# Last attention in blocks of 32 columns by four rows with 176 keys, its bias tables on GpSimd's queue, and a new order at the two ends of the state-space pipeline

## What is computed

```python
rows = S // GRID_W                    # 256 // 64 = 4
kh = min(NA_KH, rows)                 # 4: every query sees all four rows
col_start = np.clip(col - kw // 2, 0, GRID_W - kw)        # kw = 16 columns of each
col_mask = (col[None, :] >= col_start[:, None]) & (col[None, :] < col_start[:, None] + kw)
s = jnp.einsum("bqhd,bjkhd->bhqjk", q_row, k_rows) * scale + bias
s = jnp.where(col_mask[None, None, :, None, :], s, -jnp.inf)
p = jax.nn.softmax(jnp.concatenate([s, s_m], axis=-1), axis=-1)   # s_m: the 16 meta keys
```

## Time and profile before

| | us |
|---|---|
| median of 3 runs (lowest, highest) | 2495.55 (2494.72, 2496.42) |
| the profiled execution | 2496.76 |
| its span, first to last instruction | 2494.7 |
| mean granted clock | 0.994 |

### The profile page before, as it was taken

The page is one execution under the profiler, slowest core; times in us unless marked ns, Lnnn a source line. Parts: engine busy times, 40 slices in busy tenths (PEclk is TensorE's granted clock), DMA queues, the critical chain, the costliest instruction groups (busy, mean ns, idle before and its releaser), DMA issues.

```text
span 2494.7 us, 53545 instructions
## 1 busy us (share of the span) xinstructions
PE 2451.5 (98%) x18774; PEld 2342.1 (94%) x18774; DVE 1808.0 (72%) x3175; ACT 1173.0 (47%) x1663; POOL 580.5 (23%) x366
## 2 busy tenths in 40 slices
PE   8999999999999999989999999999999999999997
PEld 8999899999999888889999999999999999999986
DVE  6877877777777655578888878888862676666765
ACT  5444444444444444455666633333544444444443
POOL 0400000000000000033324257777777110001100
PEclk9999999999999999999999999999999999999999
DMA  8544655555555666665545545555455645545544
GB/s 275 189 165 136 209 170 186 184 186 184 186 184 194 195 186 186 199 207 160 181 161 166 173 138 175 174 171 193 170 169 176 187 158 168 169 158 164 166 138 140
DMA packets 159417, 441.32 MB, mean 177 GB/s; under 512 B 39475, under 2 KB 54236, under 8 KB 159212
## 3 DMA queue, kind: packets, MB, share of 16 engines
q1 hardware_dynamic: 156156, 428.15, 52.2%
q0 software_dynamic: 3184, 12.14, 1.6%
HBM read 438.05 MB, written 11.09 MB: 180 GB/s over the span
## 4 chain that ended last, share of the span: by engine, by line
PE 79%; DVE 9%; issue 5%; ACT 4%; DMA 1%; DVEq 1%; POOL 1%; ACTq 0%; SPq 0%; POOLq 0%
PE bank L1069 19%; PE bank L1070 19%; PE bank L1071 19%; PE bank L1064 10%; PE bank L1065 5%; DVE wlo L1495 3%; ACT whi L608 2%; PE bank L1302 1%; PE bank L1413 1%; ACT cv L781 1%; ACT cg L781 1%; PE bank L1394 1%; DVE cg L1802 1%; DVE cg L1805 1%; DVE cv L1802 1%
## 5 line engine op out<-in xcount | busy, mean ns | idle before, releaser
L1069 PE MATMUL bank<-xhl,whi 128*128 128x256 f32 (+1 forms) x4492 | 1294.3, 288 | 7.0 <-POOL wlo L563 3.3
L1070 PE MATMUL bank<-xhl,whi 128*128 128x256 f32 (+1 forms) x4492 | 1282.4, 285 | 0.0
L1071 PE MATMUL bank<-xhl,wlo 128*128 128x256 f32 (+1 forms) x4492 | 1281.5, 285 | 0.0
L608 ACT CAST whi<-raw 128x1024 fp32r<-128x1024 f32 x784 | 810.6, 1044 | 649.9 <-PE bank L1071 527.8
L1495 DVE TENSOR_TENSOR wlo<-raw,whi 128x1024 fp32r<-128x1024 f32 x624 | 766.6, 1239 | 239.1 <-ACT whi L608 235.2
L1069 PEld LDWEIGHTS bank<-xhl,whi 128*128 128x128 f32 x4492 | 851.0, 189 | 17.6 <-issue 9.5
L1071 PEld LDWEIGHTS bank<-xhl,wlo 128*128 128x128 f32 x4492 | 851.0, 189 | 0.0
L1070 PEld LDWEIGHTS bank<-xhl,whi 128*128 128x128 f32 x4492 | 848.5, 189 | 0.8 <-issue 0.2
L563 POOL TENSOR_TENSOR wlo<-raw,whi 128x1024 fp32r<-128x1024 f32 x160 | 383.5, 2405 | 141.5 <-ACT whi L608 141.4
L1064 PE MATMUL bank<-fhl,whi 128*128 128x512 f32 x928 | 329.5, 399 | 0.3 <-DVE wlo L1495 0.3
L1065 PE MATMUL bank<-fhl,wlo 128*128 128x256 f32 x960 | 264.4, 281 | 0.0
(11 more groups left out here) (278 smaller groups left out, 2530.4 us busy)
## 6 DMA issues: line engine op xcount, KB each, us to landing
raw<-w_up SPq DMA_DIRECT2D x176, 512.0 KB, 4.1
raw<-w_na SPq DMA_DIRECT2D x128, 512.0 KB, 3.5
raw<-w_ssm SPq DMA_DIRECT2D x96, 512.0 KB, 3.5
raw<-w_glu SPq DMA_DIRECT2D x96, 512.0 KB, 3.4
raw<-w_down SPq DMA_DIRECT2D x80, 512.0 KB, 3.7
raw<-w_qkv SPq DMA_DIRECT2D x48, 512.0 KB, 3.6
raw<-w_mix SPq DMA_DIRECT2D x32, 512.0 KB, 3.7
raw<-w_outa SPq DMA_DIRECT2D x32, 512.0 KB, 3.4
```

Source lines behind the costliest of these rows:

```text
L608: A.copy(whi[s][:, :], raw[s][:, :]).then_inc(sem("hi_done"), 1)
L1069: T.matmul(out, wh, mh[:, o:o + n], start=head, stop=False)
L1070: T.matmul(out, wh, ml[:, o:o + n], start=False, stop=False)
L1071: ins = T.matmul(out, wl, mh[:, o:o + n], start=False, stop=last)
```

## The change

It changes three things.

**The last attention's blocks.** A query block is now 32 columns of the grid by all four rows. Since a query sees 16 columns, such a block needs 40 columns of each row: 160 keys, and 16 meta keys, 176 in all (`NK`). They are kept as 120 (three rows, `NR`) and 56 (meta keys and the fourth row). `nscores`, `nturn`, `nvalues`, the softmax and the turning of v follow that; q is put into the order of blocks as it leaves PSUM, and the output back into that of rows in `pair_out`. `keyed` takes v and k out of PSUM with three products instead of one. The factor 0.5 of the output moves into `rv`, the 0.125 of q into `rq`, both made once.

**The bias tables.** GpSimd issues their loads, eight DMAs a pair of 32 partitions each, from its own queue right behind the adds of the pair before; SP's wait and four issues for each pair are gone. The adds are six a pair, of 40, 120 and 160 columns.

**The two ends of the state-space pipeline.** At the start PE does `xbc` 6 ahead of the turning of `dtx` and `acs`, `ssd` 1 ahead of `similarity`, 2 and 3 ahead of `turning`, and each of chunks 4 to 7 ahead of its `outputs`. ACT does casts 1 and 2 ahead of the exponentials and cast 3 between them, with one table load less; DVE does its work for slot 0 in another order. At the end two `glu` chunks instead of four stand between the `outputs`, behind the second and the fourth.

The core of the diff:

```diff
+NK, NR, NC = 176, 120, 40
@@ SP, last attention
-                sp.wait_ge(sem("chunk_done"), chunk("na", 0, 0) + RING)
-                sp.wait_ge(sem("btr_free"), i * 2 + 2)
-                for h in range(2):
-                    for half in range(2):
-                        rows = nrows[bass.ds(i * 2 + h, 1), 1 - half:7 - half, 63:63 + 64 * (P - 1)]
...
@@ GpSimd
+            def tables(i):
+                for h in range(2):
+                    for r in range(4):
...
+                        G.dma_start(btr[32 * r:32 * r + 32, 192 * h:192 * h + 192].rearrange(
+                            "c (r n) -> c r n", r=4), rows).then_inc(sem("btr_in"), 16)
+            def biases(i):
+                pool.wait_ge(sem("btr_in"), i * 128 + 128)
                 pool.wait_ge(sem("btm_free"), i + 1)
...
+                        if b_ == 0:
+                            G.tensor_tensor(btm[:, o + NR + META:o + NK], from_[:, 3, :], m_[:, 3, :], ADD)
+                        r_ = (3, 4)[b_]
+                        ins = G.tensor_tensor(btm[:, o:o + r_ * NC].rearrange("p (r n) -> p r n", r=r_),
+                                              from_[:, 0:r_, :], m_[:, 0:r_, :], ADD)
                     ins.then_inc(sem("btr_free"), 1)
+            biases(0)
+            with pool.Fori(1, NPAIR) as i:
+                pool.wait_ge(sem("btr_free"), i * 2 + 2)
+                tables(i)
+                biases(i)
@@ PE, state-space stage
-            for j in range(6):
+            for j in range(7):
                 stream_x("xbc", 0, j)
             pe.wait_ge(sem("acs_ready"), 1)
...
                 for v in range(4):
+                    if begin:
+                        chunk_(4 + v)
                     outputs(S, v)
-                    if end:
-                        stream_x("glu", 0, v)
-                    else:
+                    if end and v % 2:
+                        stream_x("glu", 0, v // 2)
+                    elif not end and not begin:
                         chunk_(4 + v)
@@ DVE, slot
                 if begin:
+                    evac_z(S, 0)
                     masked(S)
-                weights(S, 0)
-                evac_z(S, 0)
-                low(S, 2)
-                turned(S)
-                weights(S, 1)
-                low(S, 3)
-                evac_z(S, 1)
+                    low(S, 2)
+                    evac_z(S, 1)
+                    low(S, 3)
+                    turned(S)
+                    weights(S, 0)
+                    weights(S, 1)
@@ PE, last attention
+                for b_ in range(2):
+                    for n, rows in enumerate((NR, NK - NR)):
+                        for h in range(2):
+                            c = (2 * b_ + n) * P + 64 * h
+                            ins = T.matmul(bank[7][64 * h:64 * h + 64, b_ * P:b_ * P + P], nvr[0:rows, c:c + 64],
+                                           nps[h][0:rows, n * SEQ + b_ * P:n * SEQ + b_ * P + P],
+                                           start=n == 0, stop=n == 1)
@@ DVE, last attention
-                V.tensor_copy(nsc[m][:, 0:META], bank[3 + m][:, 0:META])
-                ins = V.tensor_tensor(nsc[m][:, META:TOK], bank[3 + m][:, META:TOK],
-                                      btm[:, o:o + SEQ], ADD)
+                ins = V.tensor_tensor(nsc[m][:, :], bank[3 + m][:, 0:NK], btm[:, o:o + NK], ADD)
```

## The result

The changed kernel takes **2478.28 us** (median of 4 runs, 2474.57 to 2479.84) beside 2495.99 us (4 runs, 2494.72 to 2497.69) of the kernel before: ratio 0.9925, 95% interval 0.9911 to 0.9940. In a second batch of 5 runs it took 2477.99 us beside 2497.04 us, ratio 0.9921 (0.9908 to 0.9935). The forecast was 2477.7 us in 2466 to 2486.

The account below looks back on a forecast made before the run. PE, busy 98% of the span, was taken to bound the kernel, so only removed PE work or PE waits pay. Start 6.1, end 6.1 and attention 5.6 us sum to 17.8 us off the 2495.55 us median: 2477.7 us, range 2466 to 2486.

Parts of the forecast that it names:

- The edits counted at nothing: Last attention: changed DVE products and copies, fewer SP waits and issues, and GpSimd's added issues and adds would cost nothing.
- Start, 6.1 us: State-space pipeline start: old waits and clock cost 15.0 us, new ones 8.9 us; gain 6.1 us, between 2 and 9.
- The chain for `outputs` 0: Pipeline start: DVE's weights 0, behind ACT's exponentials, cast 3, its wlo and `turned`, ready at 1126.4; PE waits 1.5 us.
- I charge one fall, 1.7 us: Pipeline start: only the 3.1 us wait before `ssd` 1 drops the clock, costing 1.7 us.
- End, 6.1 us: Pipeline end: earlier high_y(1) removes the 3.3 us wait for GpSimd's wlo and 2.8 us of clock; at least 3 us.
- the clock's term: Pipeline end: the clock of 0.50 behind the wait for GpSimd's wlo costs 2.8 us, which the change saves.
- Attention, 0.35 us a pair: Last attention, PE's work: `nturn` -0.43, value transposes +0.11, `nscores` -0.05, `nvalues` +0.02; x 16 = 5.6 us.
- the 0.15 us for a change of rows: `nvalues`: three changes between 120- and 56-row blocks at 0.15 us each add 0.45 us a pair.
- the forecast's price of a pass: `nscores`: each of 8 passes costs a transpose's 0.108 us for its 128-column weight load, 0.86 us in all.
- "No drain": Rival: row changes in `nvalues` cost nothing, 7.2 us more, 2470.5; with `nscores` by columns too, 2466; chance 0.2 for both.
- "A wait takes the wait's place": Rival, pipeline start: DVE and ACT set it; if exponentials or taps slip a chunk, gain 2 us, 2481.8; chance 0.15.
- GpSimd's chain: Rival, last attention: issues, landing and adds take 29.1 us, outlasting a 28.0 us pair and stopping PE; 2500 us; chance 0.04.

Follow-up runs that it names:

- six executions: Profiles of the same new start: changed kernel twice, start alone, mirrored row order, 120 rows everywhere, tables issued by SyncE; stage 3.3 to 6.9 us shorter than before.
- two others with the old end: The kernel before with the new pipeline start alone, 2489.82 us; the changed kernel with pipeline start and end put back, 2489.97 us.
- two runs to the hundredth: Changed kernel with the second block's row counts mirrored (120, 56, 56, 120), 2473.72 us; changed kernel with `nvalues` at 120 rows everywhere, 2471.55 us.
- all nine profiles: The six executions plus changed kernel with evacuation ahead of `low` 3 (2476.31 us), that with 120 rows and SyncE tables (2467.95), and the latter with earlier cast (2466.48).

## Why the prediction was right

**What bounds the kernel.** Right: what paid was work taken from PE and waits of PE that went. The edits counted at nothing on DVE and SyncE were at nothing, and GpSimd's queue cost 0.4 to 0.7 us once, in the first pair, which I had not looked at.

**Start, 6.1 us.** Right in the median (6.4 us alone, in an interval of 5.0 to 11.0), too high by 2.8 us in the first profile. Step by step, forecast and the changed kernel's profile (matmul starts apart less 0.13 us): `xbc` 6, 1.2 and 1.3; `ssd` 1, 3.1 and 2.8; `turning`, 1.1 and 1.2 (under 0.5 in three of six executions); `outputs` 0, 1.5 and 2.1; `similarity`, 0.3 and 1.1 us. The chain for `outputs` 0 left out that `low` 3 waits 0.86 us for ACT's cast before the evacuation behind it can begin, and the price of `similarity` had no row under it. The step that failed in this profile is "I charge one fall, 1.7 us": there were two. And the sum is built wrongly there: I added the half clock at `ssd` 1 to the wait before the `turning`, where the one hides in the other.

**End, 6.1 us.** Mechanism right. high_y(1) was forecast at 1450.0 us and began at 1444.86, where the trace is 4.6 us ahead of the one before: 1449.4. GpSimd's wlo never made PE wait, DVE did not become the bound, and the clock stayed at 1.00. In the first pair of profiles the clock's term was right (2.8 us) and the wait 3.4 for 3.3; what the forecast had at nothing is PE's own order, 0.6 us. The term that doesn't hold over executions is the clock's: 2.8 us was read from one, and two others with the old end lost 1.4 and 1.6 us.

**Attention, 0.35 us a pair.** It is 0.44. `nturn` and the transposes of the values came out as written. `nvalues` took 1.47 us for 1.44 before, forecast +0.02, and the 0.15 us for a change of rows is confirmed by two runs to the hundredth. `nscores` went from 1.12 to 1.03 us, -0.09 for -0.05. Its matmuls begin unevenly, some 0.06 us after the pass before, but the records of its weight loads (PEld) begin 0.11 us apart from the first pass to the last: the forecast's price of a pass held, and what was 0.04 us too dear is what stands around the passes. The remaining 0.04 us a pair I can't place; 0.03 of it lies in the two chunks between `nturn` and `nvalues`. The last pair gave 1.2 us, since besides its share a wait of 0.5 us for DVE's softmax is gone there, whose rows are a third shorter; in the pairs before it PE has other work. The other 0.2 us stay open.

**The rivals.** "No drain" fell: the price of a change is real, and its 7.2 us could only be had by avoiding the changes, at 2471.55 us where the rival had 2470.5. "A wait takes the wait's place" came half true, in the executions with 3.3 and 3.8 us. GpSimd's chain was over 12 us away from mattering. As to the rule that I named beside it, the Trainium skill (DMA: Bandwidth & Descriptors, SWDGE vs HWDGE vs iDMA) has GpSimd's descriptor writing locked out by DVE while DVE runs in its two-port mode: the 128 issues took 0.552 us each, 0.64 us at most, with DVE busy 72% of the span, and no row shows one held up. Whether DVE was in that mode during an issue no run here shows.

**Part of the hit is luck.** Against the traces the start was 2.8 us too high, the end 0.7 (most of it PE's order) and the attention 1.5 us too low, and 1.3 us came from a clock that did not fall at 41 us, where nothing was changed.

## What to carry to other kernels

Put small matmuls of one row count behind one another, or fill them up with zero rows: a change between 120 and 56 rows cost 0.15 us here, and the zeros in rows that a matmul didn't need cost nothing once they were written in idle time of DVE. Moving chunks between other work changes PE's own time too, here by 0.6 us with no wait involved; count the changes of kind before and after. A term for the clock read from one execution is one draw of several: read the same place in every profile at hand before pricing it, and don't add a half clock to the next wait for another engine. Where PE is ahead of two engines, moving one of their steps forward moves the wait; take out what stands idle in their own queues (a low half that waits for a cast, a cast that waits for a transfer).

## What the chip showed that I had not expected

- The price of a change of rows is paid over two passes: 0.20 and 0.153 us in place of 0.102 us each, so the distance at the change shows only two thirds of it. Changes between 120 and 56 columns of weights in transposes cost nothing (0.109 us each).
- The starts of small matmuls can mislead: in `nscores` some came 0.06 us after the pass before, but the loads of 128 columns of weights came 0.11 us apart throughout, and these set the length of the group.
- The same wait of 2.8 us was followed by 3.4 us at half clock in four executions of the six in the table, by 6.8 us in one, and by none in one; in all nine profiles that have it, by 3.4 us in five, 6.8 us in one and none in three.
- Adds of GpSimd made a short DVE operation at the same moment 0.55 us long instead of 0.29, and a long one 1.45 instead of 1.23.
